# Weights stationary over 320 tokens in the gate and branch sections, and probability copies ahead of the exponentials, in a hybrid retention, attention and expert step

## The chip, the cores and the metric

The kernel runs on one core of one Trainium2 chip. A core has the matrix engine TensorE (PE; its weight loads are shown as a queue of their own, PEld), VectorE (DVE), ScalarE (ACT), GpSimd (POOL) and SyncE (SP), which issues most DMA transfers. The metric is the device time of one execution in microseconds, the median of the runs.

## What is computed

One layer for 512 latent tokens and 128 context tokens, 640 in all, with 1024 channels. Cut to what matters here:

```python
h = rmsnorm(x, n1) * (1.0 + sc1) + sh1
rq, rk, rv, rg, dq, dk, dv, gr, gd = split(h @ w_in)          # 8192 columns
o_r = head_groupnorm(retention_forward + retention_backward)
ret_out = (silu(rg) * o_r) @ w_ret_o
p = softmax(q @ k.T * scale);  a = p[:, 0] - lam * p[:, 1];  o_d = a @ v     # 8 heads, two halves each
diff_out = (rmsnorm(o_d) * subln_g * (1 - lam_init)) @ w_diff_o
merged = sigmoid(gr) * ret_out + sigmoid(gd) * diff_out
x = x + g1 * (merged @ w_o)
h2 = rmsnorm(x, n2) * (1.0 + sc2) + sh2
x = x + g2 * moe(h2)          # 32 experts, two per token
```

## The kernel before, in words

The 640 tokens are five tiles of 128 (the last one is the context). Channels are eight chunks of 128 (`KC`). Every large product is a *section* of 512 output columns (`rq`, `rk`, `rv0` ... `gr0`, `gr1`, `gd0`, `gd1`, ..., `wr0`, `wr1`, `wd0`, `wd1`, `wo0`, `wo1`), and a section is two *units* of 256 columns. Weights and inputs are split into a high and a low part of reduced precision (fp32r), and a product is the sum of high x high, high x low and low x high, so that a *block*, one token tile of one unit, is 8 x 3 = 24 matmuls: 128 tokens stationary, 256 weight columns moving (`dense_item` in the TensorE program, L865 to L883). The result lies with tokens on partitions. A unit has five blocks.

The input of a section must lie with channels on partitions. `("T4", what, tile, half)` makes four transposes on TensorE; ACT or DVE (in turns, `final_engine`) copies them, scaled, to `left[what]`, and `("split", ...)` makes the high part on ACT (`high_part`, L1336 to L1339) and the low part on DVE (`low_part`, L1663 to L1668). `what` is `h` for the normalised input, `o` for the gated retention output, `od` for the attention output, `m` for the merged result. `("cv", i)` is the same split for the weights of unit i, on ACT (L1366) and DVE (L1729); it stands behind the third block of the unit before. SP loads the weights of unit i + 2 when unit i has ended (`load_w`, L597 to L601).

The order of all this is a list written out by the program, `plan`; every engine walks through it and does its part, in order. Blocks and transposes use two PSUM banks in turns, so that one waits until the one before the last is read (`freed`).

Differential attention runs in two halves of four heads, 20 steps (head, tile) each, and blocks are dealt out among the steps: 40 blocks of the sections gr and gd to the first half, two per step, and 20 of wr to the second half, one per step. A step in `plan` is: `("S", s)`: scores on PE (L1036), maxima on DVE (L1793, L1794), two exponentials on ACT (L1393), then on DVE the combination of the two distributions (L1806); `("AT", s-1)`: transposes of the combined probabilities of the step before on PE (L1050) and their copies on ACT (L1399, L1400; L1402 in the short step of the context tile); then the blocks; `prep`, transposes of keys and queries of the next head; `("PV", s-1)`: product with the values on PE (L1066, L1062), read by ACT (L1261 and L1410). `("H", h)` is the normalisation of a head on POOL (L2040 to L2042). ACT walks in this order, so in step s it makes the exponentials of s and then the copies of s-1.

The gates gr and gd are computed in the first half, go through tanh on ACT and are stored to DRAM (`gate_out`, L653 to L660); gr comes back block by block during wr (`load_gate`), gd as a whole when wr has ended (L755). wr and gr are multiplied into `merge` (L1636); wd adds to it with gd (L1646, L1649). Behind the second half stand, in this order: the transposes of od, two tiles ahead of the blocks of wd0; wd0 and wd1; the transposes of merge (`m`), two tiles ahead of the blocks of wo0; wo0 and wo1 with the router. When attention has ended SP asks for x, rows for the router and the weights of two experts (`residual`, `load_expert`), ahead of the weights of the later units.

## Time and profile before

| | us |
|---|---|
| median of 3 runs | 1314.54 (1313.31 to 1319.37) |
| the profiled execution, its own time | 1315.77 |
| its span, first to last instruction | 1313.9 |
| TensorE busy (8087 matmuls) | 1131.1, 86% |
| VectorE busy | 495.6, 38% |
| ScalarE busy | 403.5, 31% |
| matmuls of the blocks, L882, share of the chain that ended last | 39% |

Busy time of PE counts overlapping matmuls once, so it says when PE has something in its pipe, not how fast it goes; for that, the start-to-start time of matmuls is read. A row of the timeline has start, duration, engine, line, operation, output and inputs, and in brackets the idle time before it and what ended it. The profile names a matmul operand by its buffer; a full-precision matmul shows as two records.

### The profile page before, as it was taken

What the parts mean: (1) busy time and instruction counts of PE and PEld (TensorE: products, weight loads), DVE (VectorE), ACT (ScalarE), POOL (GpSimd) and SP (SyncE); (2) the same over time, 40 slices, a digit from 0 to 9 for tenths busy, and PEclk for the clock granted to TensorE, in tenths of its full rate; (3) what the DMA queues carried; (4) which work ended last, traced back from release to release, by engine and by line L of the source; (5) the groups of instructions that cost most, each with busy time, mean ns of one, the idle gap of its engine ahead of it and who ended that gap; (6) DMA issues with size and microseconds to landing.
All of it is one profiled execution on the core that took longest, in us unless ns stands there. A gap on an engine that the chain in (4) does not pass through costs nothing.

```text
span 1313.9 us, 19321 instructions
## 1 busy us (share of the span) xinstructions
PE 1131.1 (86%) x8087; PEld 916.5 (70%) x8087; DVE 495.6 (38%) x897; ACT 403.5 (31%) x870; POOL 92.4 (7%) x103
## 2 busy tenths in 40 slices
PE   2799999989998999999998888799895789777773
PEld 0488899989987888899996777699895333222221
DVE  0531114573343443442526545445547311111116
ACT  2532222211233545453225544421322121111113
POOL 0000001121000000000000000000001111110001
PEclk9799999999999999999999999899998799999996
DMA  8555632221321231223222111481316989999956
GB/s 302 220 170 204 224 98 65 65 60 46 105 65 41 61 93 61 75 80 109 65 73 69 53 48 49 158 319 65 129 33 254 381 346 419 421 421 421 421 241 240
DMA packets 90276, 222.32 MB, mean 169 GB/s; under 512 B 9881, under 2 KB 64962, under 8 KB 74706
## 3 DMA queue, kind: packets, MB, share of 16 engines
q1 hardware_dynamic: 85298, 209.60, 43.6%
q0 software_dynamic: 4608, 10.49, 2.1%
q8 instruction: 61, 1.00, 0.3%
q10 hardware_dynamic: 288, 1.05, 0.2%
q14 instruction: 21, 0.17, 0.0%
HBM read 206.40 MB, written 21.00 MB: 173 GB/s over the span
## 4 chain that ended last, share of the span: by engine, by line
PE 61%; DMA 13%; DVE 8%; ACT 8%; issue 6%; SPq 2%; POOL 1%; ACTq 0%; DVEq 0%; POOLq 0%
PE ps L882 39%; DMA arena<-in_moe_w_up 8%; PE ps L1112 6%; PE ps L1036 3%; PE ps L1066 3%; ACT arena L1393 2%; PE ps L1125 2%; DMA w_loaded<-in_w_in 2%; ACT w_high L1366 2%; DVE w_low L1729 2%; PE ps L1050 1%; PE ps L849 1%; DVE mx L1793 1%; DVE mx L1794 1%; DMA w_loaded<-in_w_diff_o 1%
## 5 line engine op out<-in xcount | busy, mean ns | idle before, releaser
L882 PE MATMUL ps<-w_high,h_high 128*128 128x256 f32 x1280 | 371.2, 290 | 10.0 <-DVE arena L1626 5.2
L882 PE MATMUL ps<-w_low,h_high 128*128 128x256 f32 x1280 | 364.5, 285 | 0.0
L882 PE MATMUL ps<-w_high,h_low 128*128 128x256 f32 x1280 | 364.4, 285 | 0.0
L882 PEld LDWEIGHTS ps<-w_high,h_high 128*128 128x128 f32 x1280 | 248.0, 194 | 24.5 <-ACT arena L1333 10.1
L882 PEld LDWEIGHTS ps<-w_low,h_high 128*128 128x128 f32 x1280 | 248.0, 194 | 0.2
L882 PEld LDWEIGHTS ps<-w_high,h_low 128*128 128x128 f32 x1280 | 247.8, 194 | 0.0
L1729 DVE TENSOR_TENSOR w_low<-w_loaded,w_high 128x2048 fp32r<-128x2048 f32 x44 | 100.8, 2291 | 177.7 <-ACT w_high L1366 177.7
L1112 PE MATMUL ps<-arena 128*64 128x512 f32 x512 | 121.3, 629 | 24.3 <-DMA arena<-in_moe_w_up 17.0
L1333 ACT COPY arena<-ps 128x256 f32<-128x256 f32 x100 | 37.2, 372 | 251.8 <-PE ps L882 251.8
L1112 PEld LDWEIGHTS ps<-arena 128*64 128x64 f32 x512 | 40.0, 145 | 103.5 <-issue 103.5
L1366 ACT CAST w_high<-w_loaded 128x2048 fp32r<-128x2048 f32 x44 | 84.0, 1908 | 62.0 <-DMA w_loaded<-in_w_o 37.4
L1393 ACT ACTIVATE arena<-ps,neg_mx 128x768 f32<-128x768 f32 (+1 forms) x80 | 62.8, 790 | 106.3 <-DVE neg_mx L1795 106.3
L1125 PE MATMUL ps<-arena 128*64 128x512 f32 x256 | 58.4, 598 | 9.8 <-ACT arena L1441 9.8
L1066 PE MATMUL ps<-arena 128*128 128x128 f32 x384 | 49.3, 278 | 13.3 <-ACT arena L1400 13.3
L1920 DVE SCALAR_TENSOR_TENSOR arena<-arena,ps 128x256 f32<-128x256 f32 x16 | 6.7, 421 | 141.1 <-ACT arena L1437 141.1
L1793 DVE TENSOR_REDUCE mx<-ps 128x1 f32<-128x768 f32 (+1 forms) x40 | 32.9, 822 | 71.5 <-PE ps L1036 71.5
L1066 PEld LDWEIGHTS ps<-arena 128*128 128x128 f32 x384 | 45.5, 192 | 16.1 <-ACT arena L1400 16.1
L1036 PE MATMUL ps<-arena 64*128 64x256 f32 (+2 forms) x288 | 53.9, 488 | 2.5 <-ACT arena L1282 1.5
L915 PE MATMUL ps<-const,arena 128*128 128x128 f32 x256 | 41.8, 294 | 11.2 <-POOL arena L2042 3.5
L882 PE MATMUL ps<-w_high,od_high 128*128 128x256 f32 x160 | 47.8, 299 | 4.1 <-DVE arena L1646 2.8
L882 PE MATMUL ps<-w_high,m_high 128*128 128x256 f32 x160 | 46.3, 289 | 2.0 <-DVE m_low L1668 0.8
L882 PE MATMUL ps<-w_high,o_high 128*128 128x256 f32 x160 | 46.9, 293 | 0.8 <-DVE o_low L1668 0.8
(268 smaller groups left out, 1664.0 us busy)
## 6 DMA issues: line engine op xcount, KB each, us to landing
w_loaded<-in_w_in SPq DMA_DIRECT2D x32, 1024.0 KB, 5.6
arena<-in_moe_w_gate SPq DMA_DIRECT2D x32, 1024.0 KB, 14.2
arena<-in_moe_w_up SPq DMA_DIRECT2D x32, 1024.0 KB, 20.5
arena<-in_moe_w_down SPq DMA_DIRECT2D x32, 1024.0 KB, 21.0
arena<-in_w_ada SPq DMA_DIRECT2D x24, 1024.0 KB, 5.7
gates<-arena SPq DMA_DIRECT2D x40, 128.0 KB, 1.7
arena<-y_rows SPq DMA_DIRECT2D x10, 512.0 KB, 8.2
arena<-in_x_sample SPq DMA_DIRECT2D x8, 512.0 KB, 10.8
```

What stands on the lines that cost most here:

```text
L849: mm = pe.matmul(B(7)[32 * j:32 * j + 32, :], ccol[:, k, :], ada_place[ada_slot(i)][:, j * N512:(j + 1) * N512], start=(k == 0), stop=(k = ...
L882: mm = pe.matmul(out[:, 0:N256], x[:, t, k * P:(k + 1) * P], w[i % 2][:, k, :], start=(k == 0 and j == 0), stop=(k == KC - 1 and j == 2))
L915: mm = pe.transpose(out[:, k * P:(k + 1) * P], src[k], ident)
L1036: mm = pe.matmul(score[c][:, lo:hi], qT[h % 2][r, t * P:(t + 1) * P], keys, start=True, stop=True, skip_group_check=True)
L1066: mm = pe.matmul(pv_out, mixedT[s % 2][:, k * P:(k + 1) * P], v, start=(k == 0), stop=(k == 5))
L1112: mm = pe.matmul(B(bank_at)[BLK * i:BLK * (i + 1), :].rearrange("p (g f) -> p g f", g=2), xgT[slot][:, k, BLK * i:BLK * (i + 1)], w_gu[e0 ...
L1125: mm = pe.matmul(B(5 + n)[BLK * i:BLK * (i + 1), :], act_aT[slot][:, k, BLK * i:BLK * (i + 1)], w_dn[e0 + i][:, k, n * N512:(n + 1) * N512 ...
L1333: free(act.copy(dst[:, t, c0:c0 + N256], src), n)
L1366: act.copy(w_hi[i % 2][:], w_raw[i % 2]).then_inc(w_rounded, 1)
L1393: act.activation(probs[:, c, 0:n], score[c][:, 0:n], ACT.Exp, bias=neg_mx[:, s % 2, c:c + 1], scale=DH ** -0.5, accum_out=den[:, s % 2, c: ...
L1729: dve.tensor_tensor(w_lo[i % 2][:], w_raw[i % 2], w_hi[i % 2][:].bitcast(F32), ALU.subtract).then_inc(w_split, 1)
L1793: dve.tensor_reduce(mx[:, 0:1], score[0][:, 0:n], AXX, ALU.max)
```

## The change

Two things.

The sections gr, gd, wr and wd (`BY_COLUMN`) turn stationary and moving operand round. The stationary operand is now 128 weight columns, the moving one tokens: 320 (`TH`) for gr, gd and wr, 384 and 256 in turns for wd. A unit has four blocks in place of five, still 24 matmuls each, and its result lies with channels on partitions. So the gates, their DRAM copy and `merge` are kept with channels on partitions, and the transposes of merge (`T4 m`) go: `merge` is split as it is, in 16 pieces (`("split", "m", chunk, part)`), one behind the next block of wd each, and the factor 0.5 is taken up in the split. The inputs `h`, `o` and `m` are stored chunk by chunk, 640 tokens each, in place of tile by tile. Within a block the order of the three products is changed to high x high, low-token x high-weight, high-token x low-weight, in all sections. Five transposes of od with their splits (heads 0 to 3) move to the end of the second attention half; the first three tiles of o are split ahead of that half. Behind attention the first block of wd0 needs three tiles of od, the second all five. The blocks of a half are dealt out by weights (5 for a block, 2 for four transposes). `cv` stands behind the second block of a four-block unit. The loads of scale2 and shift2 are asked for behind the last block of wd1. Several buffers of the expert stage get other places.

In attention the exponentials are an entry of their own, `("E", s)`, behind `("AT", s-1)`: ACT makes the copies of the transposed probabilities of step s-1 first and then the exponentials of step s.

```diff
+TOK = NT * P
+TH = TOK // 2
...
+        BY_COLUMN = ("gr", "gd", "wr", "wd")
+        LAST = lambda s: 3 if s[:2] in BY_COLUMN else PT
+
+        def block_of(s, j, hh):
+
+            lo, n = ((0, 3 * P), (3 * P, 2 * P))[j % 2] if s[:2] == "wd" else (TH * (j % 2), TH)
+            return 4 * int(s[2]) + 2 * hh + j // 2, slice(lo, lo + n), n
...
-            for t in range(NT):
+            for t in range(LAST(s) + 1):
                 out.append(("mm", s, t, hh))
-                if t == 2 and i + 1 < len(UNITS):
+                if t == LAST(s) // 2 and i + 1 < len(UNITS):
...
-            products = sum(item[0] == "mm" for item in work)
+            weight = lambda item: 5 if item[0] == "mm" else 2 if item[0] == "T4" else 0
+            products = sum(weight(item) for item in work)
             share, k = [[] for _ in mine], 0
             for item in work:
-                k += item[0] == "mm"
-                share[max(k - 1, 0) * len(mine) // products].append(item)
+                share[min(max(k, 0) * len(mine) // products, len(mine) - 1)].append(item)
+                k += weight(item)
             for j, s in enumerate(mine):
                 h, t = steps[s]
                 plan.append(("S", s))
                 if j:
                     plan.append(("AT", s - 1))
+                plan.append(("E", s))
                 for item in share[j]:
...
+        half_of = lambda what, t, half: [("T4", what, t, half), ("split", what, t, half)]
         split_o = lambda t: [("split", "o", t, half) for half in range(2)]
-        for item in split_o(0):
+        for t in range(3):
+            for item in split_o(t):
+                emit(item)
+        first = unit("wr0", 0)
+        first[1:1] = split_o(3) + split_o(4)
+        attention(1, first + unit("wr0", 1) + section("wr1") + [x for t in range(NT) for x in half_of("od", t, 0)])
+        plan.append(("att_end",))
+        opening = unit("wd0", 0)
+        opening[1:1] = half_of("od", 3, 1) + half_of("od", 4, 1)
+        m_piece = None
+        for item in [x for t in range(3) for x in half_of("od", t, 1)] + opening + unit("wd0", 1) + section("wd1"):
             emit(item)
-        first = []
-        for item in unit("wr0", 0):
-            first += [item] + (split_o(item[2] + 1) if item[0] == "mm" and item[2] + 1 < NT else [])
-        attention(1, first + unit("wr0", 1) + section("wr1"))
-        plan.append(("att_end",))
-        for n, item in enumerate(with_left("od", unit("wd0", 0)) + unit("wd0", 1) + section("wd1")):
-            emit(item)
-            if item[0] == "mm" and item[1:] in (("wd0", 1, 1), ("wd0", 2, 1), ("wd0", 3, 1), ("wd0", 4, 1)):
-                plan.append(("W", item[2] - 1))
-            if item == ("mm", "wd1", 2, 0):
-                plan.append(("LB",))
-        for item in with_left("m", unit("wo0", 0)) + unit("wo0", 1):
+            if item[0] == "mm":
+                if m_piece:
+                    emit(m_piece)
+                m_piece = ("split", "m", block_of(*item[1:])[0], item[2] % 2)
+                if item[1] == "wd0" and item[3] == 1:
+                    plan.append(("W", item[2]))
+                if item == ("mm", "wd1", 2, 0):
+                    plan.append(("LB",))
+        emit(m_piece)
+        for item in section("wo0"):
...
+        def splits_needed(s, t):
+
+            if s == "rq":
+                return split_n[("h", t, 1)]
+            if s == "wo0":
+                return split_n[("m", KC - 1, 0 if t < 3 else 1)]
+            what, tiles_in = ("o" if s == "wr0" else "od"), (range(3) if t % 2 == 0 else range(NT))
+            return max(split_n[(what, u, half)] for u in tiles_in for half in range(2))
...
-                    elif item == ("T4", "m", PT, 1):
+                    elif n == last_of["wd1"]:
...
-                        pe.wait_ge(x_split, split_n[(kind, t, 1)])
+                        pe.wait_ge(x_split, splits_needed(s, t))
                     _, x_hi, x_lo = left[kind]
+                    _, sl, width = block_of(s, t, hh) if s[:2] in BY_COLUMN else (0, slice(t * P, (t + 1) * P), N256)
                     for k in range(KC):
-                        for j, (x, w) in enumerate(((x_hi, w_hi), (x_hi, w_lo), (x_lo, w_hi))):
-                            mm = pe.matmul(out[:, 0:N256], x[:, t, k * P:(k + 1) * P], w[i % 2][:, k, :],
-                                           start=(k == 0 and j == 0), stop=(k == KC - 1 and j == 2))
+                        for j, (x, w) in enumerate(((x_hi, w_hi), (x_lo, w_hi), (x_hi, w_lo))):
+                            if kind == "od":
+                                tokens = x[:, sl.start // P:sl.stop // P, k * P:(k + 1) * P]
+                            else:
+                                tokens = x[:, k, sl]
+                            if s[:2] in BY_COLUMN:
+                                fixed, moving = w[i % 2][:, k, (t // 2) * P:(t // 2 + 1) * P], tokens
+                            else:
+                                fixed, moving = tokens, w[i % 2][:, k, :]
+                            mm = pe.matmul(out[:, 0:width] if kind != "od" else out[:, 0:width].rearrange("p (t n) -> p t n", n=P),
+                                           fixed, moving, start=(k == 0 and j == 0), stop=(k == KC - 1 and j == 2))
...
-                wait_freed(act, where[("T4", what, t, half)])
-                c = slice(N512 * half, N512 * (half + 1))
-                act.copy(left[what][1][:, t, c], left[what][0][:, t, c]).then_inc(x_rounded, 1)
+                whole, high = piece(what, left[what][0], t, half), piece(what, left[what][1], t, half)
+                if what == "m":
+                    act.wait_ge(merged, merged_at[(t, half)])
+                    scale_copy(high, whole, 0.5).then_inc(x_rounded, 1)
+                else:
+                    wait_freed(act, where[("T4", what, t, half)])
+                    act.copy(high, whole).then_inc(x_rounded, 1)
...
-                elif e[0] == "S":
+                elif e[0] == "E":
...
                 elif kind == "wd":
-                    c0 += N256 * hh
+                    cb, sl, width = block_of(s, t, hh)
                     dve.wait_ge(pe_dense, n + 1)
                     dve.wait_ge(ld_gd, 16)
-                    m = merge_t[:, n % 2, :]
+                    m = gated[:, 0:width]
                     if n_merged[0]:
                         dve.wait_ge(merged, n_merged[0])
                     n_merged[0] += 1
-                    free(dve.scalar_tensor_tensor(out=m, in0=gd_t[:, t, c0:c0 + N256], scalar=1.0, in1=src[:, 0:N256],
+                    free(dve.scalar_tensor_tensor(out=m, in0=gd_t[:, cb, sl], scalar=1.0, in1=src[:, 0:width],
                                                   op0=ALU.add, op1=ALU.mult), n)
                     wait_freed(dve, n)
-                    dve.tensor_tensor(merge[:, t, c0:c0 + N256], merge[:, t, c0:c0 + N256], m, ALU.add).then_inc(merged, 1)
+                    dve.tensor_tensor(merge[:, cb, sl], merge[:, cb, sl], m, ALU.add).then_inc(merged, 1)
                 elif kind == "wo":
                     c0 += N256 * hh
...
+                if what == "m":
+                    dve.scalar_tensor_tensor(out=low, in0=whole, scalar=0.5, in1=high.bitcast(F32), op0=ALU.mult,
+                                             op1=ALU.subtract).then_inc(x_split, 1)
+                else:
+                    dve.tensor_tensor(low, whole, high.bitcast(F32), ALU.subtract).then_inc(x_split, 1)
...
```

## Rows read from the trace of the kernel before

**Rows 1.** The page, parts 1 (busy time by engine) and 4 (shares of the chain).

```profile
PE 1131.1 (86%) x8087; PEld 916.5 (70%) x8087; DVE 495.6 (38%) x897; ACT 403.5 (31%) x870; POOL 92.4 (7%) x103
...
PE ps L882 39%; DMA arena<-in_moe_w_up 8%; PE ps L1112 6%; PE ps L1036 3%; PE ps L1066 3%; ACT arena L1393 2%; PE ps L1125 2%; DMA w_loaded<-in_w_in 2%; ACT w_high L1366 2%; DVE w_low L1729 2%; PE ps L1050 1%; PE ps L849 1%; DVE mx L1793 1%; DVE mx L1794 1%; DMA w_loaded<-in_w_diff_o 1%
```

**Rows 2.** Stretches: length, busy time by engine (instructions), granted clock, DMA share, GB/s.

```profile
418.00:603.00 185.00, 178.59 (x1425) 163.26 (x1424) 77.15 (x127) 91.32 (x233) 7.92 (x9) 1.00 0.24 71
692.90:843.40 150.50, 128.21 (x962) 108.38 (x963) 80.58 (x152) 75.03 (x197) 7.89 (x9) 1.00 0.15 49
843.40:921.00 77.60, 69.59 (x524) 66.79 (x523) 38.02 (x65) 17.47 (x22) 2.82 (x3) 0.91 0.59 220
921.00:945.60 24.60, 21.11 (x161) 18.65 (x159) 15.85 (x25) 10.69 (x16) 0.00 (x0) 1.00 0.37 119
```

**Rows 3.** The chain that ended last: start, duration, what.

```profile
174.69 28.79 PE ps L882 x240
```

**Rows 4.** Timeline of PE, full-precision matmuls of the retention output.

```profile
302.77 0.60 PE L1012 MATMUL ps<-arena 128*128 128x256 f32 x2
303.20 0.59 PE L1015 MATMUL ps<-arena 128*128 128x256 f32 x2
```

**Rows 5.** Waits, second attention half: engine, line, releaser: us, times, longest.

```profile
PE ps L1066 <- ACT arena L1400: 13.3, 12, 1.9
PE ps L1062 <- ACT arena L1402: 3.2, 3, 1.1
PE ps L1050 <- ACT ps L1410: 2.8, 5, 0.9
```

**Rows 6.** Timeline of all engines, one step of the second attention half.

```profile
718.04 0.84 PE L1050 MATMUL ps<-const,arena 128*128 128x128 f32 x6 [0.94 <-ACT ps L1410]
719.04 0.95 DVE L1793 TENSOR_REDUCE mx<-ps 128x1 f32<-128x768 f32 x1
721.09 0.90 ACT L1393 ACTIVATE arena<-ps,neg_mx 128x768 f32<-128x768 f32 x1 [3.19 <-DVE neg_mx L1795]
721.60 0.60 PE L915 MATMUL ps<-const,arena 128*128 128x128 f32 x4
722.86 0.58 ACT L1399 COPY arena<-ps 128x512 f32<-128x512 f32 x1
723.32 0.39 ACT L1400 COPY arena<-ps 128x256 f32<-128x256 f32 x1
723.76 0.49 PE L1066 MATMUL ps<-arena 128*128 128x128 f32 x2 [1.56 <-ACT arena L1400]
```

**Rows 7.** Groups by line and form, 843.4 to 945.6: count, busy, mean ns, idle before.

```profile
L1729 DVE TENSOR_TENSOR w_low<-w_loaded,w_high 128x2048 fp32r<-128x2048 f32 x5 | 11.4, 2288 | 6.1 <-ACT w_high L1366 6.1
L1646 DVE SCALAR_TENSOR_TENSOR arena<-arena,ps 128x256 f32<-128x256 f32 x20 | 8.4, 419 | 23.6 <-PE ps L882 23.4
L1668 DVE TENSOR_TENSOR od_low<-od_whole,od_high 128x512 fp32r<-128x512 f32 x10 | 6.9, 692 | 10.9 <-ACT od_high L1339 10.9
L1339 ACT CAST od_high<-od_whole 128x512 fp32r<-128x512 f32 x10 | 6.2, 619 | 13.7 <-DVE od_whole L1597 13.5
L1261 ACT ACTIVATE od_whole<-ps,cols 128x512 f32<-128x512 f32 x5 | 3.4, 684 | 1.8 <-PE ps L915 1.8
```

**Rows 8.** Timeline of PE behind attention and at the first block of wd1.

```profile
847.42 3.04 PE L915 MATMUL ps<-const,arena 128*128 128x128 f32 x12 [3.54 <-POOL arena L2042]
...
890.54 0.58 PE L882 MATMUL ps<-w_high,od_high 128*128 128x256 f32 x1 [2.48 <-DVE arena L1646]
```

**Rows 9.** The chain that ended last, in the wd sections.

```profile
850.81 5.39 PE ps L882 x24
...
873.10 12.80 DMA w_loaded<-in_w_diff_o
```

**Rows 10.** Timeline of SP's DMA issues behind attention.

```profile
840.52 0.58 SPq L755 DMA_DIRECT2D arena<-gates  x1
```

**Rows 11.** Timeline of PE in the first unit of wo0.

```profile
928.63 1.34 PE L915 MATMUL ps<-const,arena 128*128 128x128 f32 x8
```

More of the change, by code:

```diff
@@ L191, in build @@
         logit_bias = at(134.75, 2 * 36).rearrange("p (s n) -> p s n", s=2)
-        scale2, shift2 = tiles(162, 2, D), tiles(170, 2, D)
-        h2 = [at(158, D), at(80, D)]
+        scale2, shift2 = tiles(182, 2, D), tiles(190, 2, D)
+        h2 = [at(178, D), at(80, D)]
         n2_row = h2[1]
@@ L505, in build, with piece @@
                 spill_at[item[1:]] = len(spill_at)
[L506 to L507 removed]
+        last_of = {s: where[("mm", s, LAST(s))] for s in SECTIONS}
+        unit_end = {n: unit_at[(item[1], item[3])] for n, item in enumerate(dense) if item[0] == "mm" and item[2] == LAST(item[1])}
+        merged_at = {}
+        for item in dense:
+            if item[0] == "mm" and item[1][:2] == "wd":
+                merged_at[(block_of(*item[1:])[0], item[2] % 2)] = len(merged_at) + 1
+        def splits_needed(s, t):
[5 more added lines that the diff above has]
+            return max(split_n[(what, u, half)] for u in tiles_in for half in range(2))
+        def piece(what, v, t, half):
+            if what == "m":
+                sl = (slice(0, 3 * P), slice(3 * P, TOK))[half]
+                return v[:, t, sl]
+            if what == "od":
+                return v[:, t, N512 * half:N512 * (half + 1)]
+            return v[:, 4 * half:4 * half + 4, t * P:(t + 1) * P]
         end_of = {i: n for n, i in unit_end.items()}
@@ L1665, in low_part @@
                 dve.wait_ge(x_rounded, split_n[(what, t, half)])
-                c = slice(N512 * half, N512 * (half + 1))
-                whole, high, low = left[what]
-                dve.tensor_tensor(low[:, t, c], whole[:, t, c], high[:, t, c].bitcast(F32), ALU.subtract).then_inc(x_split, 1)
+                whole, high, low = (piece(what, v, t, half) for v in left[what])
+                if what == "m":
+                    dve.scalar_tensor_tensor(out=low, in0=whole, scalar=0.5, in1=high.bitcast(F32), op0=ALU.mult,
+                                             op1=ALU.subtract).then_inc(x_split, 1)
+                else:
+                    dve.tensor_tensor(low, whole, high.bitcast(F32), ALU.subtract).then_inc(x_split, 1)
             def router_input(t):
```

85 lines of the change are left out of this document (39 added, 46 removed).

## The prediction

> **What bounds the kernel now.** I read the page first, then a table of stretches, then the chain that ended last, then single steps. The page says that TensorE (PE) is busy 86% of the span [rows 1]; ScalarE (ACT) and VectorE (DVE) are below 40%, so the question is where PE works and where it waits. The stretches [rows 2] name the parts that the change touches: the first attention half (418 to 603 us: PE 178.6 of 185), the second attention half (692.9 to 843.4: PE only 128.2 of 150.5), the wd sections (843.4 to 921) and the start of wo (921 to 945.6). From about 1000 us on, the experts follow; they start when the router is through and wait for weights of their own (8% of the chain that ended last [rows 1]), so what is won before 1000 us is won at the end. Three limits are to be seen. First, the matmul stream itself: 240 matmuls take 28.79 us in the chain [rows 3], 120 ns from one start to the next, with nothing in between. Second, in the second attention half PE waits for ACT. Third, around the wd sections PE waits for a chain of transposes, copies and splits, and for one weight load.
>
> **The stream: 256 columns become 320.** Of each of 16 units (8 gate, 4 wr, 4 wd) the 5 blocks of 24 matmuls with 256 columns go, and 4 blocks of 24 come, of 320 columns in the gate and wr units and of 384 and 256 columns in turns in the wd units. The columns in all are the same (1280 per k-step and product), so all depends on what 120 ns consists of. 256 columns at 2.4 GHz are 106.7 ns; 13 ns remain. Is that a cost of each matmul or the time of the weight load, that hides the stream? The full-precision matmuls L1012 to L1017, which also load 128 weight columns each, tell: two of them every 0.433 us [rows 4], 216.7 ns each. They stream 256 columns, at two cycles a column 213.3 ns, so the fixed part is 3.4 ns when the stream is long. Hence I read 120 ns as the floor of the weight load and take 320 columns at 133.3 + 3.6 = 137 ns, 384 columns at 160 + 3.6 = 163.6 ns, 256 columns at 120 ns as now. No row has a matmul of this precision of more than 256 columns, so the bounds: not under 120 ns, what 256 columns take, and above either 133.3 + 13.3 = 146.6 ns (the 13 ns are a cost of each) or 149.9 ns (pure proportion). I take 137 since the rows of L1012 differ only in precision. A block then takes 24 x 0.137 = 3.29 us where it took 2.88, a gate or wr unit 13.15 instead of 14.4, a wd unit 2 x 24 x (0.1636 + 0.120) = 13.6.
>
> The Trainium skill ("TensorE: Matmul & The Clock Gate", section "Back-to-back issue gap") gives the gap of isolated matmuls as columns over 2.4 GHz plus 2.5 ns. By that rule 256 columns would take 109 ns and 320 would take 136, 5 x 109 against 4 x 136, and the swap would win nothing; in the sum below that takes out 12 x 1.25 + 4 x 0.8 = 18 us and gives 1298. The 120 ns of [rows 3] disagree with it at 256 columns; at 320 the rule gives what I take, and no row can say. The same section says that in a real stream the weight loads and the matmuls set the spacing together, and that is what [rows 3, 4] look like.
>
> **First attention half.** 40 blocks were 115.2 us and become 32 of 3.29, 105.3. PE is busy 178.6 of 185 us there [rows 2], so this falls on the path: **-9.8 us** (bounds -2.7 by 146.6 ns, -23 by 120 ns). Twelve steps get two blocks and eight get one, where all had two; a one-block step is still about 7.3 us of PE work, more than the 5.7 us of scores, maximum and exponentials, so no wait comes in. The gate's ACT copies get longer (320 columns) but fewer, 32 for 40; they lie beside PE. Fewer and larger gate stores: nothing, the DMA share is 0.24 there [rows 2].
>
> **Second attention half.** Here each step has one block, and PE waits 13.3 us for the second copy of the transposed probabilities (L1400) and 3.2 us for its short form L1402 [rows 5]. One step shows why [rows 6]: PE's transposes of the probabilities end at 718.9, but ACT first waits for the maxima (exponentials 721.09 to 722.9) and only then makes the two copies, until 723.7; PE, done with block and transposes at 722.2, starts the product L1066 at 723.76. With the copies ahead of the exponentials they run in ACT's 3.19 us of idle time (they are done at about 719.9), and the exponentials still start when the maxima come: VectorE needs 2.1 us from the scores on (719.04 to 721.09), transposes and copies (0.58 + 0.39 us) need 1.7. What is late next is the next step's scores, which wait for the exponentials; but the product (1.5 us) stands before them, and the exponentials end 1.0 us before the copies ended, so they are done in time. So all is won: **-16.5 us**. Against it: 16 blocks cost 0.41 us more each, +6.6. Four steps lose their block (work is dealt out by weights now: steps 9, 17, 18, 19 of 20) and become bound by the chain of scores, maxima and exponentials (1.5 + 2.1 + 1.9 + 0.2 = 5.7 us) or of transposes and copies: I get -2.3, -1.0, -1.4, -1.9, in sum -6.6 (worked out from the durations of [rows 6]). Into the last three steps go five transposes of od with their copies and splits, on ACT about 0.7 + 0.6 us each [rows 7]; in step 18 two of them stand ahead of the read of the product for which the next transposes wait: +2.5. The splits of o: six instead of two stand before the half on ACT and DVE, so the copies of the first keys and queries come 4 x 0.6 = 2.4 us later, and four more stand ahead of the second step's maxima: +1.2; together +3.6. Sum -16.5 + 6.6 - 6.6 + 2.5 + 3.6 = **-10.4**; I take **-9.5**, for a waited semaphore that moves (L1050 behind the read of the product, 2.8 us of waits now [rows 5]) may grow. Bounds: -4 (the waits half recovered) and -14.
>
> **wd sections.** Five of the ten transposes of od, each with copy and split, have moved into attention. What remains behind it: the five of the second half, for which PE waits until 847.42 on GpSimd (POOL) as now [rows 8]. Before the first block three transposes with three copies and splits stand, a row of about 4.4 us from 847.4, so the block starts at about 851.8 where it started at 850.81; PE is at 1.2 GHz until about 856 either way (24 matmuls take 5.39 us from 850.81 [rows 9]). Then one bubble of 3.6 us for the last two tiles, where now three shorter ones stand, about 5 us together. With blocks of 6.1, 2.9, 3.9, 2.9 the first unit ends at 871.2 (now 873.1), the second at 884.8. Its successor waits for weights: their load is issued at 873.10 and lands 12.8 us later behind two experts' weights, then its conversion on ACT and DVE follows (the DVE part alone 2.3 us), and PE idles 2.48 us until 890.54 [rows 7 to 9]. In the change the 2.5 MB of gd gates are asked for when wr ends, which is now three steps (about 18 us) before attention ends, not 3 us before (840.52 [rows 10]); so the loads of x and the experts have the queue for themselves, and the weights can land by 880. Then the next section starts at 885.1, and lasts 27.5: end at 912.6 instead of 920.95, -8.3. If the load lands where it does now, the end is at 918.5, -2.5. I take **-7**.
>
> **m.** The ten transposes of merge, their copies and their place in the row disappear. Now 24.7 us lie between the end of wd1 and the second unit of wo0 (921 to 945.6 [rows 2]), of which 14.4 are matmuls; the rest is transposes (8 in 1.34 us) and waits for them [rows 11]. In the change the scale is in the split, which is made block by block while wd runs; after the last block only two DVE steps of 0.42 us [rows 7], the split of the last column block that stands behind them (0.55, estimated from 0.69 for 512 columns) and latencies remain, 1.6 us, before wo starts. 16 splits instead of ten, 0.4 to 0.6 us on each of ACT and DVE, lie beside blocks of 2.9 and 3.9 us. So 24.7 becomes 16.1: **-8.6** (bounds -6 and -9). The loads of scale2 and shift2 come before this stretch, at low DMA share: nothing. The change in the order of the three products in the token-stationary sections: the same loads and columns, nothing. New places of buffers for the experts: nothing.
>
> **Sum.** -9.8 - 9.5 - 7 - 8.6 = -34.9. The profiled execution took 1315.77 us (span 1313.9), which is 1.2 above the median of 1314.54. 1315.77 - 34.9 = 1280.9, or 1279.7 against the median: **1280 us**.
>
> **Rivals.** (a) *The 13 ns are a cost of each matmul, or the time goes by columns.* Then 320 columns take 146.6 to 149.9 ns. 48 blocks x 24 x 9.6 to 12.9 ns = 11.1 to 14.9 us are lost, 8 blocks of 384 columns at 9.6 to 16 ns give 1.8 to 3.1: 1293 to 1298. For it: at 256 columns nothing tells them apart. Against it: [rows 4]. 12%. (b) *The wait moves.* The copies go first, but the exponentials, or the read of the product behind conversions (2.3 us on DVE), take its place, and half of 16.5 us and all of the gain in the wd sections stay out: 1280 + 8 + 6 = 1294. For it: L1050 waits already in both halves. Against: ACT idles 3.19 us before the exponentials in the step shown [rows 6]. 12%. (c) *Weight load only:* 320 columns stay at 120 ns; 48 x 24 x 17 ns = 19.6 us more is won: 1260. Against it: no row streams faster than a column per cycle. 2%. (d) *Slower.* Matmuls of this precision drop to two cycles per column beyond 256 columns, as L1012 runs: 320 columns take 270 ns. 48 x 24 x 133 ns = 153 us, and 8 x 24 x (323 - 164) ns = 31 us: 1464. It decides from the point at which a 320-column matmul takes more than about 137 + 35/1.15 = 167 ns. For it: the trace has no such matmul of over 256 columns, and a moving operand of three pieces is new. Against: 512 columns of full precision show no such edge. 4%.
>
> **Chances and range.** Forecast 70%, by its own bounds 1271 to 1289. Range 1269 to 1298: it takes in (a) and (b) and leaves out (c), (d) and what lies beyond the bounds. A measurement of this kernel can tell about 0.5%, 6.5 us, from no change. Faster by more than that: the forecast, (a), (b), (c), 0.96, less 0.02 for (a) and (b) at once (1298 + 14 = 1312, the same): 0.94; same 0.02; slower (d) 0.04.
>
> **What would show it.** The start-to-start time of 320-column matmuls: 137 ns right, 147 or more (a), 270 (d). First attention half shorter by 10 us, with PE still over 95% busy. In the second half, waits of L1066 for L1400 near zero, and no new line above 3 us in their place; else (b). The wait for w_diff_o before wd1 under 1 us, the load of the gates far ahead of those of x. From the end of wd1 to the first block of wo0 under 2 us. Wrong would be a time above 1298, which would mean that the stream or the dealing of the work costs more than any row here says.

## The result, and the profile after

The changed kernel takes 1304.26 us (median of 4 runs, 1304.06 to 1305.04) where the kernel before takes 1314.77: the ratio is 0.992, with a 95% interval of 0.990 to 0.994. It is faster by 10.5 us, where 34.9 were forecast, and lies 6 us above the upper end of the range (1269 to 1298). The sign was right, the size wrong. Of the executions timed for the experiments below, one of experiment 2 (1670 us) and one of the kernel before beside experiments 1 to 4 (2253 us) were disturbed and are left out.

The page of the changed kernel, parts 1 and 4 (as [rows 1] of before; the blocks of matmuls, L882 before, are L939 now, the scores L1090, the transposes of the probabilities L1104, the product L1120, the low parts of the splits L1724):

```profile
PE 1122.6 (86%) x7663; PEld 909.9 (70%) x7663; DVE 491.9 (38%) x886; ACT 405.7 (31%) x863; POOL 94.7 (7%) x103
...
PE ps L939 43%; DMA arena<-in_moe_w_up 8%; PE ps L1166 7%; PE ps L1090 3%; PE ps L1120 3%; PE ps L1179 2%; DMA w_loaded<-in_w_in 2%; ACT arena L1448 2%; PE ps L1104 2%; PE ps L897 1%; ACT w_high L1421 1%; PE ps L969 1%; DVE w_low L1785 1%; DVE mx L1849 1%; DVE mx L1850 1%
```

PE is as busy as before in its share, with fewer and longer matmuls (7663 for 8087). Where the time went is to be seen in the table of stretches, cut at the same events as in [rows 2]: the first attention half, the second (from its first scores to its last product), the wd sections, and the start of wo up to its second unit (length, busy time by engine, granted clock, DMA share, GB/s):

```profile
413.00:595.20 182.20, 179.03 (x1250) 162.76 (x1251) 78.88 (x128) 93.86 (x225) 7.91 (x9) 1.00 0.23 71
687.10:842.20 155.10, 132.58 (x884) 112.79 (x884) 82.97 (x151) 79.40 (x201) 10.38 (x9) 0.94 0.18 61
842.20:917.90 75.70, 64.73 (x406) 63.32 (x406) 37.84 (x65) 19.19 (x29) 2.63 (x3) 0.88 0.52 186
917.90:934.10 16.20, 14.72 (x123) 14.75 (x124) 7.30 (x14) 2.32 (x2) 0.00 (x0) 1.00 0.55 195
```

Against the profiled execution of before:

| stretch | before, us | after, us | difference | forecast |
|---|---|---|---|---|
| up to the first half | 415.2 | 413.0 | -2.2 | 0 |
| first attention half | 187.9 | 182.2 | -5.7 | -9.8 |
| way into the second half | 3.4 | 5.4 | +2.1 | +2.4 |
| second attention half | 150.5 | 155.1 | +4.6 | -11.9 |
| wd sections | 77.5 | 75.7 | -1.8 | -7 |
| start of wo | 24.7 | 16.2 | -8.5 | -8.6 |
| all behind it | 368.25 | 368.25 | 0 | 0 |

(The three sections between the attention halves take 86.4 us in both. The forecast of -9.5 for the second half is shown in two rows, with the six early splits of o in the first of them.) The first row isn't the change's: the kernels of experiments 1 and 8 both equal the kernel before up to this point, and one reached the first half at 412.84, the other at 415.4. So a single execution places this stretch within 2.5 us, and smaller differences there mean nothing.

The matmul of 320 columns. The chain that ended last, in the base part (256 columns), and in one step of the first half (two blocks, then one, of 24 matmuls with 320 columns):

```profile
174.02 28.79 PE ps L939 x240
...
424.11 7.04 PE ps L939 x48
...
435.22 3.52 PE ps L939 x24
```

28.79 / 240 is 120 ns, as before; 7.04 / 48 is 146.7 ns, where I took 137. The timeline of PE in wd1 has the matmuls of 384 columns:

```profile
882.25 0.34 PE L939 MATMUL ps<-od_high,w_high 128*128 128x384 f32 x1
...
882.77 0.33 PE L939 MATMUL ps<-od_high,w_high 128*128 128x384 f32 x1
...
884.33 0.33 PE L939 MATMUL ps<-od_high,w_high 128*128 128x384 f32 x1
```

From the first of these to the last there are 12 starts in 2.08 us, 173.3 ns each. 120, 146.7, 173.3: 26.7 ns for each 64 columns, which is the stream at 2.4 GHz (the granted clock is 1.00 in all three places), and 13.3 ns on top at each width. What the 13.3 ns are made of, no run here shows.

The waits in the second attention half and the 5.4 us ahead of it (engine, line, what ended the wait: us, times, longest), which answer to [rows 5]:

```profile
PE ps L1104 <- ACT ps L1465: 9.5, 6, 4.2
PE ps L939 <- DVE o_low L1724: 7.4, 1, 7.4
PE ps L969 <- ACT arena L1331: 2.9, 1, 2.9
PE ps L1090 <- ACT arena L1448: 2.3, 4, 0.8
PE ps L1120 <- ACT arena L1455: 1.5, 2, 0.9
```

The wait that the change meant to remove is nearly gone: L1120 for L1455 (L1066 for L1400 in [rows 5], 13.3 us) is 1.5 us. Two others stand in its place. The larger single one is near the start. The chain there:

```profile
700.23 1.02 DVE arena L1862
701.25 0.62 DVE o_low L1724 x2
...
702.37 1.30 DVE o_low L1724 x2
...
703.80 5.21 PE ps L939 x24
```

The second block of wr0 streams all tokens of its half, so it needs the last two tiles of o, whose four splits the plan places behind the maxima, the exponentials and (on DVE, at 700.23) the combination of the second step. On DVE they end at 703.67. PE had nothing else it could do for 7.4 us, and the block behind the wait runs in part at half clock: 5.21 us where others take 3.52, with a granted clock of 0.70 from 703.8 to 709.1.

The other is at the end of the half, where the transposes of od with their copies and splits now stand. All engines, ahead of the transposes of the probabilities L1104:

```profile
830.00 0.75 DVE L1651 TENSOR_SCALAR od_whole<-ps,cols 128x512 f32<-128x512 f32 x1
830.77 0.62 ACT L1394 CAST od_high<-od_whole 128x512 fp32r<-128x512 f32 x1 [2.30 <-DVE od_whole L1651]
831.30 0.68 ACT L1315 ACTIVATE od_whole<-ps,cols 128x512 f32<-128x512 f32 x1
...
832.13 0.34 ACT L1465 ACTIVATE ps<-ps,rden 128x128 f32<-128x128 f32 x1
...
832.73 0.66 PE L1104 MATMUL ps<-const,arena 128*128 128x128 f32 x2 [4.22 <-ACT ps L1465]
```

ACT waits 2.30 us for a copy of od on DVE, which itself stands behind the attention's work there; the read of the product (L1465), for which PE waits, comes after ACT's split and the next tile's copy.

### The profile page after: what moved, and what is told of

It is laid out like the page before. It is cut to its first block, busy times and chain, and to the rows that moved or that the text cites. A ratio compares the mean times of both kernels' runs of the same rounds, so it can differ in the third digit from the quotient of the medians.

```text
span 1302.3 us, 18423 instructions
## 1 busy us (share of the span) xinstructions
PE 1122.6 (86%) x7663; PEld 909.9 (70%) x7663; DVE 491.9 (38%) x886; ACT 405.7 (31%) x863; POOL 94.7 (7%) x103
## 4 chain that ended last, share of the span: by engine, by line
PE 65%; DMA 12%; DVE 7%; issue 7%; ACT 6%; SPq 2%; POOL 1%; ACTq 0%; DVEq 0%; POOLq 0%
PE ps L939 43%; DMA arena<-in_moe_w_up 8%; PE ps L1166 7%; PE ps L1090 3%; PE ps L1120 3%; PE ps L1179 2%; DMA w_loaded<-in_w_in 2%; ACT arena L1448 2%; PE ps L1104 2%; PE ps L897 1%; ACT w_high L1421 1%; PE ps L969 1%; DVE w_low L1785 1%; DVE mx L1849 1%; DVE mx L1850 1%
## 5 line engine op out<-in xcount | busy, mean ns | idle before, releaser
L939 PE MATMUL ps<-w_high,h_high 128*128 128x256 f32 x960 | 278.1, 290 | 9.8 <-DVE arena L1679 5.2
L939 PE MATMUL ps<-w_high,h_low 128*128 128x256 f32 x960 | 273.1, 284 | 0.0
L939 PE MATMUL ps<-w_low,h_high 128*128 128x256 f32 x960 | 273.0, 284 | 0.0
L939 PEld LDWEIGHTS ps<-w_high,h_high 128*128 128x128 f32 x960 | 185.6, 193 | 24.0 <-ACT arena L1384 10.1
L939 PEld LDWEIGHTS ps<-w_high,h_low 128*128 128x128 f32 x960 | 185.8, 194 | 0.2
L939 PEld LDWEIGHTS ps<-w_low,h_high 128*128 128x128 f32 x960 | 185.6, 193 | 0.0
L939 PE MATMUL ps<-h_high,w_high 128*128 128x320 f32 x256 | 80.7, 315 | 0.0
L939 PE MATMUL ps<-h_high,w_low 128*128 128x320 f32 x256 | 79.1, 309 | 0.0
L939 PE MATMUL ps<-h_low,w_high 128*128 128x320 f32 x256 | 79.1, 309 | 0.0
L1090 PE MATMUL ps<-arena 64*128 64x256 f32 (+2 forms) x288 | 55.3, 498 | 3.9 <-ACT arena L1448 2.3
L1120 PE MATMUL ps<-arena 128*128 128x128 f32 x384 | 48.8, 277 | 1.5 <-ACT arena L1455 1.5
L939 PE MATMUL ps<-o_high,w_high 128*128 128x320 f32 x128 | 41.6, 325 | 8.8 <-DVE o_low L1724 7.4
L939 PEld LDWEIGHTS ps<-h_high,w_high 128*128 128x128 f32 x256 | 48.3, 189 | 0.3 <-issue 0.3
```

The costliest lines, as they stand in the source:

```text
L939: mm = pe.matmul(out[:, 0:width] if kind != "od" else out[:, 0:width].rearrange("p (t n) -> p t n", n=P), fixed, moving, start=(k == 0 and ...
L1090: mm = pe.matmul(score[c][:, lo:hi], qT[h % 2][r, t * P:(t + 1) * P], keys, start=True, stop=True, skip_group_check=True)
L1120: mm = pe.matmul(pv_out, mixedT[s % 2][:, k * P:(k + 1) * P], v, start=(k == 0), stop=(k == 5))
```

## The experiments

Ratios, with their 95% intervals, are against the kernel before, beside which each kernel was timed; its median was 1313.5 to 1315.1 us in these three rounds. Differences to the changed kernel compare medians of two rounds, so a microsecond or two of them means nothing.

**1. The copies first, and nothing else.** The kernel before, with the exponentials as an entry of the plan of their own, behind the copies of the transposed probabilities:

```diff
                 if j:
                     plan.append(("AT", s - 1))
+                plan.append(("E", s))
...
-                elif e[0] == "S":
+                elif e[0] == "E":
```

> The kernel before with one part of the change alone: ACT makes the copies of the transposed probabilities ahead of the exponentials. Theory A (the copies' place is worth its waits, 16.5 us in the second attention half, and the rest of the change gave them back): 1299, between 1296 and 1302; L1066's wait for the second copy under 3 us. Theory B (the wait only moves to the exponentials and to the read of the product): 1310 or more, and a new wait of PE of over 8 us in the second half.

Measured: 1300.37 us (1299.31 to 1304.83), ratio 0.991 (0.988 to 0.993). Its second half lasts from 690.55 to 826.11, 135.6 us where before took 150.5; its first half is 187.9 us, as before. The waits that remain in its second half:

```profile
PE ps L1051 <- ACT ps L1411: 3.7, 3, 1.4
PE ps L1037 <- ACT arena L1394: 3.4, 5, 1.0
PE ps L1051 <- DVE arena L1807: 2.1, 3, 1.0
```

So this one line of the plan brings 14.4 to 15 us by itself, near the 16.5 of the forecast, and more than the whole change brings. Theory A came, theory B did not: no line of these waits is for the copies, and the longest is 3.7 us in all. All the rest of the change together costs about 4 us by the medians (1304.26 against 1300.37; the intervals overlap), though its m part alone gains 8.5.

**2. The changed kernel with the exponentials first again.**

```diff
-                elif e[0] == "E":
+                elif e[0] == "S":
```

> The changed kernel with the exponentials ahead of the copies again, everything else kept. Theory A: the waits for the copies come back, 12 to 16 us: 1316 to 1320, slower than the kernel before. Theory B: under 1308.

Measured: 1319.36 us (1316.97 to 1320.14), ratio 1.003 (1.001 to 1.004), 15.1 us above the changed kernel, as theory A had it. The wait for the copies is back:

```profile
PE ps L1120 <- ACT arena L1455: 11.4, 7, 3.5
PE ps L939 <- DVE o_low L1724: 7.2, 1, 7.2
```

The order of the copies is worth the same, 15 us, with either shape of the blocks. The rest of the change alone, as it stands, makes the kernel no faster but 0.3% slower.

**3. The splits of o one block earlier.** The changed kernel, where the last four splits of o are dealt out as if they stood one block ahead, which puts them into the first step:

```diff
-                share[min(max(k, 0) * len(mine) // products, len(mine) - 1)].append(item)
+                at_k = k - 5 if item[0] == "split" and item[1] == "o" else k
+                share[min(max(at_k, 0) * len(mine) // products, len(mine) - 1)].append(item)
```

> The changed kernel, but the splits of the last two tiles of o are dealt to the step of the block that they stand behind (ahead of the second step's scores), not to the step after. Theory A (PE idles 7.4 us for them because they stand behind the second step's exponentials and combination, and runs 3 us longer at 1.2 GHz after it): 1295, between 1292 and 1298, and the wait for o_low under 3 us. Theory B (the conversions keep ACT and DVE busy for as long wherever they stand, so PE waits elsewhere): 1301 or more.

Measured: 1298.34 us (1294.78 to 1300.61), ratio 0.988 (0.985 to 0.991). The wait is down from 7.4 to 2.0 us, and the second half from 155.1 to 148.3:

```profile
PE ps L1105 <- ACT ps L1466: 9.2, 6, 4.2
...
PE ps L940 <- DVE o_low L1725: 2.0, 1, 2.0
```

The median is 0.3 us above what theory A allowed at most, and 2.7 under B's bound; the wait that left is the one named, and 6 us of the time went with it.

**4. The transposes of od behind attention.**

```diff
-        attention(1, first + unit("wr0", 1) + section("wr1") + [x for t in range(NT) for x in half_of("od", t, 0)])
+        attention(1, first + unit("wr0", 1) + section("wr1"))
         plan.append(("att_end",))
+        for t in range(NT):
+            for item in half_of("od", t, 0):
+                emit(item)
```

> The changed kernel, but the five transposes of the first half of od with their splits stand behind attention again (they fall in the 3.8 us in which PE waits for POOL), and the blocks are dealt over all 20 steps. Theory A (in the last steps they stand ahead of the reads of the product, PE waits 4.2 and 2.9 us for these, and falls to 1.2 GHz): 1299, between 1296 and 1301. Theory B (they cost the same wherever they are): 1304 to 1306.

Measured: 1297.95 us (1296.04 to 1298.69), ratio 0.988 (0.986 to 0.990), in the range of theory A. Of the 9.5 us of waits for the read of the product 2.3 are left in the second half:

```profile
PE ps L1107 <- ACT ps L1468: 2.3, 4, 0.9
```

The second half is 146.2 us, 8.9 shorter (the new dealing of the blocks is in this, as no run changes one alone); the wd sections are 80.3, 4.6 longer, less than the 8.2 us that five half tiles take at 1.64 us each (read in the trace of experiment 6, where this row of transpose, copy and split is run through eight times from 826.6 to 839.9), and the wait of 3.8 us for GpSimd that stood there is gone. The transposes were moved into attention to take them off the path; at its end they were on it.

**5. 512 and 128 columns for 320 and 320.** The gate and wr blocks of the changed kernel stream the first 512 tokens, and then the last 128, with buffers and the splits ahead of the first block to match; the matmuls are as many, and the columns too:

```diff
-            lo, n = ((0, 3 * P), (3 * P, 2 * P))[j % 2] if s[:2] == "wd" else (TH * (j % 2), TH)
+            lo, n = ((0, 3 * P), (3 * P, 2 * P))[j % 2] if s[:2] == "wd" else ((0, N512), (N512, P))[j % 2]
```

> The changed kernel with blocks of 512 and 128 tokens in place of 320 and 320 in the gate and wr sections; the number of matmuls and the columns are the same. The splits of o: four tiles ahead of the half, one behind the first block. Theory A (a matmul of this precision costs its columns at 2.4 GHz and 13.3 ns more, whatever its width): 512 columns 226.6 ns, 128 columns 66.6 ns from start to start, and a time like that of the changed kernel, 1300 to 1306. Theory B (120 ns at 256 columns is the floor of the weight load): 128 columns take 107 to 120 ns, 24 blocks x 24 x 40 to 53 ns = 23 to 31 us more: 1325 to 1335.

Measured: 1330.78 us, ratio 1.012 (1.009 to 1.015): 26.5 us above the changed kernel. The chain in the first half, a block of 512, a pair of both widths, and a block of 128 columns:

```profile
539.50 5.49 PE ps L939 x24
545.00 0.44 PE ps L969 x4
...
549.07 8.14 PE ps L939 x48
...
560.73 2.63 PE ps L939 x24
```

5.49 / 24 is 228.8 ns (213.3 + 15.5; other blocks of it 5.46, 227.5 ns), and 2.63 / 24 is 109.6 ns where the columns are 53.3. Both theories were half right, and the time is the one of B. From 256 to 512 columns a matmul costs its columns and 13 to 15 ns, so the 120 ns of [rows 3] aren't a floor that a longer stream hides. At 128 columns theory A's 66.6 ns don't hold. One width below 256 can't say what does: a floor of about 110 ns, or two cycles a column, as the full-precision records of [rows 4] have it (216.7 ns for 256 columns). For the second speaks that the four transposes at 545.00, also of 128 columns but of full precision, take 0.44 / 4 = 110 ns each too; no run separates them. A pair costs 338 ns in place of 293; 24 pairs of matmuls in each of 24 pairs of blocks make 26 us, the difference found.

**6. Both moves together (3 and 4).** The edits of experiments 3 and 4 in one kernel.

> The changed kernel with both moves: splits of o with the block that they stand behind, the first half of od behind attention. Theory A (two separate stalls): 1290, between 1287 and 1293, faster than both kernels. Theory B (one stall covers the other): 1296 or more.

Measured: 1290.54 us (1289.54 to 1292.33), ratio 0.982 (0.980 to 0.985). The waits in its second half, which lasts 136.7 us where the changed kernel took 155.1:

```profile
PE ps L1124 <- ACT arena L1459: 3.8, 4, 0.9
PE ps L1108 <- ACT ps L1469: 2.3, 4, 0.9
PE ps L943 <- DVE o_low L1728: 1.7, 1, 1.7
```

With the two misplaced groups gone, the second half is nearly as short as with the copies first alone (135.6), and shorter than forecast (150.5 - 11.9 = 138.6): the dearer blocks (16 x 0.64 = 10.2 us) must be paid by something, which I take to be the four steps without a block. The half is 18.4 us shorter than in the changed kernel; the wd sections, with all ten transposes of od, are 79.2 us for 75.7. In sum 13.7 us of the missing 24.4 are found. The row of od remains; the timeline of PE at the first and the second block of wd0:

```profile
840.01 0.66 PE L943 MATMUL ps<-od_high,w_high 128*128 128x384 f32 x1 [3.63 <-DVE od_low L1728]
...
850.56 0.55 PE L943 MATMUL ps<-od_high,w_high 128*128 128x256 f32 x1 [3.30 <-DVE od_low L1728]
```

**7. The transposes ahead of the splits.** Experiment 6, where each transpose of od stands one place ahead of the split before it, and those of the last two tiles ahead of the first block, so that only their splits stand behind it:

```diff
-        for t in range(NT):
-            for item in half_of("od", t, 0):
-                emit(item)
+        order = [("od", t, half) for half in range(2) for t in range(NT)]
+        turned = [("T4",) + order[0]]
+        for i, x in enumerate(order):
+            turned += ([("T4",) + order[i + 1]] if i + 1 < len(order) else []) + [("split",) + x]
         opening = unit("wd0", 0)
-        opening[1:1] = half_of("od", 3, 1) + half_of("od", 4, 1)
+        opening[1:1] = [x for x in turned if x[0] == "split" and x[2] > 2 and x[3] == 1]
+        turned = [x for x in turned if x not in opening]
-        for item in [x for t in range(3) for x in half_of("od", t, 1)] + opening + unit("wd0", 1) + section("wd1"):
+        for item in turned + opening + unit("wd0", 1) + section("wd1"):
```

> The kernel after with the o splits one block earlier, all ten transposes of od behind attention, and now each transpose one place ahead of the split before it; the last four transposes also stand ahead of the first block of wd, only their splits behind it. Theory A: what ate the gain of the wd sections is the serial row transpose, copy, high part, low part (1.64 us for each half tile in the trace of the run with both moved, from 827.3 to 839.9), which the weight-stationary blocks must await for three whole tiles, and the bubble of 4.6 us behind the first block. Run ahead, a half tile costs what ACT or VectorE need, about 1.1 us: the first block starts 3 to 4 us earlier and the bubble of 4.6 us goes: 1290.5 - 3.5 - 4.0 = 1283 (1280 to 1286). Theory B: GpSimd's scaling or the engines' own work set the row: no less than 1288.

Measured: 1284.57 us (1281.28 to 1285.93), ratio 0.976 (0.974 to 0.978): 30.5 us under the kernel before, and the fastest of all. The same two places:

```profile
837.97 0.41 PE L945 MATMUL ps<-od_high,w_high 128*128 128x384 f32 x1 [1.03 <-DVE od_low L1730]
...
844.93 0.36 PE L945 MATMUL ps<-od_high,w_high 128*128 128x256 f32 x1 [2.54 <-DVE od_low L1730]
```

From the last product (826.42) to the first block are 11.6 us for 14.7; the block takes 4.44 us for 5.95; and the gap between the blocks is 2.5 for 4.6 us. What the clock did is to be seen in the stretches of the first and of the second block (length, busy time by engine, granted clock, DMA share, GB/s):

```profile
837.90:842.50 4.60, 4.43 (x24) 4.14 (x24) 0.65 (x2) 0.62 (x1) 0.00 (x0) 1.00 0.76 144
844.90:848.00 3.10, 3.07 (x18) 3.10 (x19) 0.00 (x0) 1.03 (x1) 0.00 (x0) 0.66 1.00 420
```

The first block runs at full clock. The second, behind the shorter gap, does not: it takes 4.44 us (844.93 to 849.37) for the 2.88 of 24 matmuls of 256 columns, so this bubble still costs its 2.5 us and 1.6 more. The wd sections last 72.7 us, 6.5 less than in experiment 6 and 4.8 less than before. Of the expectation's two parts the first was right (3 to 4 us); the second gap didn't vanish, since the block ends at 842.41, 1.5 us sooner after its start, and the last of the four splits behind it at 844.79 on DVE.

**8. The same order in the kernel before.** Experiment 1 with each transpose of od and m one place ahead of the split before it, and nothing weight-stationary:

```diff
-            return out
+            if what == "h":
+                return out
+            turned = [x for x in out if x[0] == "T4"]
+            ahead, k = [], 0
+            for x in out:
+                if x[0] == "T4":
+                    more = turned[k:k + 2] if k == 0 else turned[k + 1:k + 2]
+                    ahead += more
+                    k += 1
+                else:
+                    ahead.append(x)
+            return ahead
```

> The kernel before with the copies first and, in the od and m rows, each transpose one place ahead of the split before it; nothing is weight-stationary. It asks how much of the gain of the m part (24.6 us to 16.2 in the changed kernel) needs the weight-stationary blocks. Theory A: most waits of the m row are the serial row, not the transposes: the row from the end of wd1 to the second unit of wo0 goes from 24.6 to about 19 us; what is won in the first unit of wd is lost to the wait for the load of w_diff_o (15 us of the chain in the run with the copies first alone): 1300.4 - 5.5 - 1 = 1294 (1291 to 1297). Theory B: the transposes and splits themselves are the cost, and only leaving them out helps: no less than 1299.

Measured: 1299.92 us (1298.81 to 1301.28), ratio 0.988 (0.986 to 0.990), against 0.991 (0.988 to 0.993) of experiment 1: no difference that this can tell. The stretch of m shrinks from 24.6 to 23.0 us, not to 19. The last pieces of its chain:

```profile
925.62 1.81 ACT w_high L1378
...
929.66 0.43 DVE arena L1671
...
930.14 0.98 PE ps L894 x6
```

Behind the last splits ACT and DVE have the conversion of the next weights, and the result of the block waits for that. The time is the one of theory B, and for this order theory A is refuted: leaving the transposes of m out, as the change does, gains 8.5 us, of which this order gives 1.6. That no other order would give more isn't shown. Between this kernel and that of experiment 7, both with the copies first and the transposes ahead, lie 15 us: so much the weight-stationary sections are worth, with all that comes with them (m without transposes, work dealt out by weights, the splits of o ahead), once PE waits for less of what they moved.

## Why the prediction was wrong, point by point

Two steps failed. The larger is in the second attention half: the terms for the moved splits of o and transposes of od (+3.6 and +2.5) counted engine time and not the wait of PE behind it, and moving both groups away again takes 18.4 us off that half (experiment 6). The other is the stream: 320 columns were taken at 137 ns and take 146.7, 13 us in all.

**The stream.** The failed step is "I read 120 ns as the floor of the weight load", drawn from L1012, whose records of 256 columns at two cycles a column have only 3.4 ns over their columns. (They aren't two matmuls every 0.433 us but the two records of one: the program makes four matmuls at L1012 for a tile, and the trace has eight records.) The row was of another precision, and the remark that it differs only in precision was the weak spot: the matmuls of this stream have 13.3 ns on top from 256 to 384 columns. That is rival (a), its 146.6 ns nearly to the digit, which I gave 12%. The term is 9.6 ns too small at 320 columns: 48 blocks x 24 x 9.6 ns = 11.1 us, and 8 x 24 x 9.7 ns = 1.9 us in wd. Experiment 5 shows that the fixed part holds up to 512 columns (13 to 15 ns), and that at 128 columns something else limits. The Trainium skill ("TensorE: Matmul & The Clock Gate", section "Back-to-back issue gap") gives the gap of isolated matmuls as columns over 2.4 GHz plus 2.5 ns. The traces agree with its slope (26.7 ns per 64 columns) and not with its constant.

**First attention half:** -5.7 where -9.8 was forecast. The blocks gave 115.2 - 32 x 3.52 = 2.6 us, the bound that I had named. The other 3 us I hadn't counted: PE waited 6.1 us for the read of the product in five places of the first half, and now waits 2.8. The first line is of before, the second of the changed kernel:

```profile
PE ps L1050 <- ACT ps L1410: 6.1, 5, 1.3
PE ps L1104 <- ACT ps L1465: 2.8, 5, 0.9
```

It goes with the new blocks and not with the order of the copies: with the copies first alone it is 6.1 us (experiment 1), with the new blocks and the exponentials first 2.8 (experiment 2). That fewer of ACT's gate copies and conversions stand ahead of the read is my reading, not tested.

**Second attention half:** the first term, -16.5 for the copies, held: 15 us alone (experiment 1) and 15 in the changed kernel (experiment 2). Rival (b) in its own terms, half of this left unwon, did not come. What failed is the pricing of where the new plan puts other work. "[F]our more stand ahead of the second step's maxima: +1.2" gave the splits of o the price of ACT's time in a queue and missed who waits for them: the second block, the first one that needs all five tiles. It costs a wait of 7.4 us and 1.7 us of half clock; moving them gave 6 us (experiment 3). And the order was the other way round: they stand behind the exponentials, not ahead of the maxima. "[I]n step 18 two of them stand ahead of the read of the product [...]: +2.5" was the right mechanism at the right place, too small: it happens in the last steps twice (4.2 and 2.9 us), and the second half is 8.9 us shorter without it (experiment 4). The block term is +10.2 instead of +6.6. That the steps without a block gain about as much as the dearer blocks cost fits (136.7 against 135.6 us, experiments 6 and 1), though no run takes them apart. The delay of the first scores by the six early splits came as forecast (+2.1 for +2.4).

**wd sections:** -1.8 for -7. Right was that the wait for the weight load goes: no load is on the chain between 842 and 917. The pieces of it that matter:

```profile
845.97 1.10 PE ps L969 x4
...
852.65 6.51 PE ps L939 x24
...
863.75 36.89 PE ps L939 x240
```

The row of three transposes took 6.7 us from 845.97 (to 852.65), not 4.4; the block 6.5 us, not 6.1; the bubble 4.6, not 3.6; and behind it the next block ran at half clock for most of its length, 4.43 us (863.75 to 868.18) for 2.9, which I had not thought of. With 1.9 us for the 384 columns these are 2.3 + 0.4 + 1.0 + 1.5 + 1.9 = 7.1 us; the stretch is 6.5 us longer than the 69.2 that I had added up. Experiment 7 gets back 6.5 us of this stretch, at the same widths, by the order alone (79.2 us in experiment 6 to 72.7, both with all ten transposes in it).

**m:** -8.5 for -8.6; two DVE steps, the last split and latencies, as worked out. The chain from the last block of wd1 to the first of wo0:

```profile
917.88 0.43 DVE arena L1699
...
918.34 0.43 DVE arena L1702
918.76 0.48 DVE m_low L1721
...
919.38 15.71 PE ps L939 x129
```

**The chances.** Rival (a) alone gives 1293 to 1298, and I took what goes wrong in the stream and what goes wrong in the second half as cases that hardly meet ("(a) and (b) at once" had 0.02). They have separate causes, and both happened: 13 us of dearer matmuls, 13.7 us of misplaced splits and transposes and about 5 us in the row of wd, less 3 us not counted on in the first half and 2 us of the run: 27 us in rough sum, where 24.4 are missing (the 13.7 count a part of the row too). A range over independent terms has to reach to their sum: the least gains that I had named for the four parts (2.7, 4, 2.5 and 6 us) already give 1299.3, above the 1298 of the range. Even so 1304.3 lies outside, since in the second half no bound allowed for a loss. That the forecast mechanisms (copies first, steps without a block, no transposes of m) can pay is to be seen from experiment 7: with these waits out of the way and the dear matmuls in it, 30.5 us are won.

## What to carry to other kernels

The fixed cost of a matmul is read from two widths of the same precision; where the trace has only one, nothing in it tells the two readings (floor or constant) apart, and the sum is made for both. Making the weights stationary means that a block needs every tile of the activations it streams: list the splits and copies that stand between those tiles and the first two blocks, on each engine's queue, before counting what the longer stream saves. A cheap change of order (copies ahead of exponentials) brought by itself nearly half of the 30.5 us of the best kernel here. And filler work did well here where PE waited anyway (for GpSimd), and badly at the end of a stretch where each read is waited for.

## What the runs showed of the hardware

Start to start, at a granted clock of 1.00, streams of this precision with a weight load each: 128 columns 109.6 ns, 256 columns 120, 320 columns 146.7, 384 columns 173.3, 512 columns 227.5 to 228.8. From 256 up it is the columns at 2.4 GHz and 13 to 15 ns. The 109.6 ns lie above that line (66.6); whether they are a floor or a lower rate is open.

Several waits cost more than their length, since PE's granted clock was at 1.2 GHz in the work behind them. The first scores of the second half took 2.96 us (1.49 elsewhere) behind waits of 2.94 and 0.74 us. The second block of wr0 took 5.21 us for 3.52, behind 7.4 us. The second block of wd0 took 4.43 us for 2.9 in the changed kernel, where PE had done eight transposes and then waited 3.3 us in the 4.6 us ahead of it, and 4.44 in experiment 7, behind a gap of 2.5 us. The first block of wd0 took 6.51 us in the changed kernel and 5.95 in experiment 6, both behind 3.6 us in which the granted clock was 0.50 already; in experiment 7, behind 1.0 us, it took 4.44 us at a granted clock of 1.00, where 24 matmuls of 384 columns are 4.16 in a row (24 x 173.3 ns). So the length of the last wait alone doesn't say what the clock will be.
